# Expert stage of a decoder layer: 28 instead of 24 of 64 experts on 64 row slots, in a period of sixteen steps

## What is computed

```python
def routed_experts(xf, idx, gates, w1_e, w3_e, w2_e):
    ...
    def run_block(args):
        e, toks, g = args
        xb = xpad[toks]
        hb = jax.nn.silu(xb @ w1_e[e]) * (xb @ w3_e[e])
        return (hb @ w2_e[e]) * g[:, None].astype(xb.dtype)
    ...

def moe(x, w_router, router_bias, w1_e, w3_e, w2_e, w1_s, w3_s, w2_s):
    ...
    _, idx = lax.top_k(jnp.where(emask, biased, -jnp.inf), TOP_K)
    w_sel = jnp.take_along_axis(scores, idx, axis=1)
    gates = w_sel / jnp.sum(w_sel, axis=-1, keepdims=True) * ROUTED_SCALE
    y = swiglu(xf, w1_s, w3_s, w2_s) + routed_experts(xf, idx, gates, w1_e, w3_e, w2_e)
```

## Time and profile before

| | |
|---|---|
| median of 3 runs | 1221.01 us |
| lowest and highest | 1220.01 and 1221.2 us |
| the profiled execution's own time | 1218.57 us |
| its span (first to last instruction) | 1216.8 us |
| mean granted clock of TensorE, share of full speed | 0.978 |
| PE busy (matmuls) | 1138.4 us, 94% |
| DVE, ACT, POOL busy | 411.7, 257.2, 176.1 us |
| bytes moved by DMA | 319.16 MB |

### The profile page before, as it was taken

The page is one execution under the profiler, slowest core; times in us unless marked ns, Lnnn a source line. Parts: engine busy times, 40 slices in busy tenths (PEclk is TensorE's granted clock), DMA queues, the critical chain, the costliest instruction groups (busy, mean ns, idle before and its releaser), DMA issues.

```text
span 1216.8 us, 21054 instructions
## 1 busy us (share of the span) xinstructions
PE 1138.4 (94%) x8302; PEld 759.3 (62%) x8302; DVE 411.7 (34%) x1016; ACT 257.2 (21%) x564; POOL 176.1 (14%) x210
## 2 busy tenths in 40 slices
PE   7999997999988999889999999999999999999964
PEld 6888645877865788657755555555655555655410
DVE  0369997122048324821121212122121121111133
ACT  1101334022041125101122222122222222222200
POOL 3120050000000000111122222122221222212100
PEclk9999998999999999999999999999999999999978
DMA  9630404034047353346999999999999999999496
GB/s 332 235 139 1 156 13 173 1 138 156 1 140 258 157 209 156 155 143 243 352 384 384 385 389 384 380 386 388 388 388 380 371 381 393 384 389 385 161 367 269
DMA packets 66313, 319.16 MB, mean 262 GB/s; under 512 B 10311, under 2 KB 16671, under 8 KB 39629
## 3 DMA queue, kind: packets, MB, share of 16 engines
q1 hardware_dynamic: 51269, 278.60, 59.9%
q0 software_dynamic: 13568, 35.48, 8.6%
q10 hardware_dynamic: 1424, 4.35, 0.9%
HBM read 300.15 MB, written 29.36 MB: 271 GB/s over the span
## 4 chain that ended last, share of the span: by engine, by line
PE 72%; DVE 14%; DMA 10%; issue 1%; ACT 1%; SPq 1%; POOL 0%; POOLq 0%; DVEq 0%
PE psum L750 65%; DVE act_mem L1704 7%; PE psum L765 7%; DMA arena<-in_w_e_dram 5%; DMA arena<-y_rows 3%; DVE mk_mem L1863 2%; DMA arena<-in_w_in_dram 1%; DMA act_mem<-x_rows,idx_x 1%; SPq L541 0%; DVE act_mem L1801 0%; DVE act_mem L1718 0%; DVE rstd L1792 0%; DVE act_mem L1799 0%; DVE act_mem L1769 0%; DMA y_rows<-act_mem,idx_y 0%
## 5 line engine op out<-in xcount | busy, mean ns | idle before, releaser
L750 PE MATMUL psum<-arena,act_mem 128*32 128x128 f32 (+6 forms) x4800 | 512.3, 363 | 6.0 <-DMA arena<-in_w_e_dram 5.1
L750 PEld LDWEIGHTS psum<-arena,act_mem 128*32 128x32 f32 (+5 forms) x4800 | 263.4, 124 | 193.8 <-issue 110.7
L750 PE MATMUL psum<-act_mem,arena 128*128 128x260 f32 (+1 forms) x1728 | 352.4, 366 | 6.0 <-ACT act_mem L1550 2.0
L750 PEld LDWEIGHTS psum<-act_mem,arena 128*128 128x128 f32 x1728 | 306.0, 192 | 49.7 <-ACT act_mem L1550 2.4
L765 PE MATMUL psum<-ident,act_mem 96*128 96x96 f32 (+8 forms) x484 | 76.8, 288 | 19.3 <-POOL ident L559 6.8
L673 POOL DMA_INDIRECT y_rows<-act_mem,idx_y x40 | 45.1, 1128 | 320.2 <-DVE idx_x L2080 170.5
L2092 DVE TENSOR_SCALAR act_mem<-psum,act_mem 96x512 f32<-96x512 f32 (+1 forms) x40 | 29.9, 748 | 155.6 <-PE psum L750 155.6
L1704 DVE SCALAR_TENSOR_TENSOR act_mem<-act_mem,wcb 128x511 f32<-128x511 f32 (+29 forms) x120 | 77.7, 728 | 0.0
L765 PEld LDWEIGHTS psum<-ident,act_mem 96*128 96x128 f32 (+8 forms) x484 | 56.5, 174 | 32.3 <-issue 8.6
L2089 DVE TENSOR_TENSOR act_mem<-act_mem,psum 128x192 f32<-128x192 f32 x35 | 12.4, 354 | 175.5 <-ACT act_mem L1560 175.5
L750 PEld LDWEIGHTS psum<-act_mem 128*96 128x96 bf16 (+4 forms) x371 | 28.5, 126 | 57.2 <-issue 51.2
(11 more groups left out here) (264 smaller groups left out, 729.2 us busy)
## 6 DMA issues: line engine op xcount, KB each, us to landing
arena<-in_w_e_dram SPq DMA_DIRECT2D x192, 1024.0 KB
arena<-y_rows SPq DMA_DIRECT2D x8, 2048.0 KB, 23.5
arena<-in_w_in_dram SPq DMA_DIRECT2D x16, 512.0 KB, 18.3
arena<-in_cache_mem_k_dram SPq DMA_DIRECT2D x8, 1024.0 KB, 9.0
arena<-in_cache_mem_v_dram SPq DMA_DIRECT2D x8, 1024.0 KB, 11.8
arena<-in_w_v_dram SPq DMA_DIRECT2D x1, 4096.0 KB, 24.5
arena<-in_w_k_dram SPq DMA_DIRECT2D x1, 4096.0 KB, 13.9
arena<-in_w_out_dram SPq DMA_DIRECT2D x1, 4096.0 KB, 13.9
```

Source lines behind the costliest of these rows:

```text
L750: return pe.matmul(out, lhsT, rhs, start=first, stop=last)
```

## The change

The period becomes sixteen steps, with seven light positions: 2, 4, 6, 9, 11, 13 and 15. Over 64 steps 28 experts are on 64 slots, and four that had 96 slots now have 64. The big steps are still the long ones among the first eight positions (`BIGS`), which are now 0, 1, 3, 5 and 7. `picked`, a small tile whose size goes with NB, has a new place. The counts in the waits of `step` that were written for NB = 8 are now computed from NB. PE's, POOL's and SP's order within a step is the same, and SP's loop over the weights isn't touched; but the prologue is sixteen steps, the loop sixteen steps that run twice, and the epilogue fifteen steps.

```diff
-NB = 8
-LIGHT = (2, 5, 7)
-HEAVY = (0, 1, 3, 4, 6)
+NB = 16
+BIGS = 8
+LIGHT = (2, 4, 6, 9, 11, 13, 15)
+HEAVY = (0, 1, 3, 5, 7, 8, 10, 12, 14)
...
 def is_big(e):
-    return isinstance(e, int) and e < NB and e % NB in HEAVY
+    return isinstance(e, int) and e < BIGS and e % NB in HEAVY
 
 
 def turned(e):
 
-    return lights(e) if isinstance(e, int) and e < NB else e - (len(HEAVY) - 1)
+    return e + 1 - sum(1 for h in HEAVY if h < BIGS and (not isinstance(e, int) or h <= e))
...
-        picked = act_mem[:, A4 + 1280:A4 + 1280 + 2 * NB].rearrange("p (n c) -> p n c", c=2)
+        picked = act_mem[:, A4 + 1820:A4 + 1820 + 2 * NB].rearrange("p (n c) -> p n c", c=2)
...
             for k in HEAVY:
-                gp.memset(bump[:, NB + k:E:NB], float(CAP - MCAP)).then_inc(s_sortc, 1)
+                gp.memset(bump[:, k if k >= BIGS else NB + k:E:NB], float(CAP - MCAP)).then_inc(s_sortc, 1)
...
-                c_step(e, k % NB, 48 * (2 * i + (k // 4 + 1)))
+                c_step(e, k % NB, 48 * (NB // 4 * i + (k // 4 + 1)))
                 if exists(e + 1):
-                    b_step(e + 1, (k + 1) % NB, 16 * (2 * i + ((k + 1) // 4 + 1)))
+                    b_step(e + 1, (k + 1) % NB, 16 * (NB // 4 * i + ((k + 1) // 4 + 1)))
```

## The result

The changed kernel takes 1228.53 us (median of 7 runs, 1224.66 to 1231.22) against 1221.01 (7 runs, 1220.01 to 1222.46): a ratio of 1.0058, interval 1.0041 to 1.0075, so about 7 us slower. In a second series it was 1227.52 against 1221.83, 1.0046 (1.0028 to 1.0064). The forecast was 1219.2 with a range of 1214 to 1225.

What follows compares the result with a forecast made beforehand. Transfers were taken to bound the expert stage, PE close behind. 3.0 + 1.84 + 0.76 − 1.9 − 1.5 − 0.4 = 1.8 us gained, so 1221.0 − 1.8 = 1219.2 us, range 1214 to 1225.

Steps and rivals of the forecast that it cites:

- The bound: Expert stage: transfers limit at 9.58 us per expert, PE close behind at 9.39; PE's saved 17.1 us counts 0.
- Rival A: Expert stage: transfers keep up, wanting 404 GB/s, so PE sets the time, 1195.6 us; chance 0.06.
- cost 1: PE's longer loop: 18 to 30 more instruction pages cost 1.9 us, at most 3.8; the jump back costs 0.
- gain 1: End of the stage: the last expert's up-projection begins when the last load lands; 3.0 us gained (2.8 to 4.6).
- Rival B: Expert stage: further pages fall on few engines, making loads late; four engines 1224.8 us, one 1247.3; chance 0.12.
- Gain 2: Near the stage's start, 588 us: light position 4 closes the DMA gap before load 7; 1.84 us gained (0 to 1.84).
- Gain 3: DMA share dips after a long PE wait, at 935 to 937 and 946 to 948 us, vanish; 0.76 us gained.
- cost 2: Expert stage: PE's recurring waits for weights leave DMA dips; two episodes cost 1.5 us (0 to 4).
- Cost 3: End of the stage: c(63) waits for a landing and begins after it; 0.4 us lost (0 to 0.9).

Runs made afterwards that it cites:

- without the jump: The changed kernel with PE's loop of two passes written out, so PE never jumps back: 1222.02 us, 1.0001.
- two jumps: The kernel before with two passes of PE's loop written out as one, sixteen steps run three times: 1235.40 us, 1.0113.
- half idle engines: The changed kernel loading only a quarter of w1 and w3 and half of w2 from expert 4 on: 1199.06 us in one run.
- half of w2: The changed kernel loading only the first half of each w2 from expert 4 on: 1204.76 us, 0.9858.

## Why the prediction was wrong

**The bound: right.** The transfers set the pace. PE's 16.7 us went into waits for weights (5.1 us before, 21.2 without the jump; 10.3 + 4.7 in the first profile, beside the stall of 6.1), and came out as time only where the loads were cut. Rival A falls: in the two profiles of the changed kernel no 100 us had more than 388 GB/s, where 404 was wanted.

**The step that failed is the last sentence but two of cost 1**: "PE now has 9.58 − 9.12 = 0.46 us to spare in each step and makes up even 5 us in eleven steps, so 0". It priced the jump back as PE's time, of which there was enough. But PE also feeds the transfers: a buffer comes free when y(e) is done. PE had no lead when it stopped, since it had just waited for its weights (0.87 us before 849.16); two loads were queued, the stall and the slow clock behind it took 8.3 us, and the queue ran down. PE caught up afterwards, by waiting for nothing for some steps. The engines' idle 4.6 us can't be caught up: in the rest of the stage they are as full as before it. By the runs the jump costs 5.5 us (changed kernel against the same without it) and 5.3 each (two jumps); 2.8 between the period of sixteen with 24 light and the written-out kernel before, all within 2 us or so of uncertainty. The bound I gave it, 5 us, was near the size of the stall, and the way it would reach the time was missed.

The rule that I named there speaks of exactly this: by the Trainium skill ("Runtime: NRT & Kernel Launch", "Instruction fetch mechanics") a taken branch out of the window stalls until its page is fetched. The trace agrees: two pages moved around each of the seven stalls, and the stall was 2.1 us beside half idle engines, 4.6 to 6.1 with full loads. I had used that rule for the number of pages alone. The kernel with the loop written out fetches as many pages as the changed one (44 against 46 in 560 to 1160 us), so the second pass of a body of some 2,900 recorded instructions fetches everything again, where one of 1,517 stays for six passes.

**Cost 1, the pages: too small.** 1.9 us was taken, 3.8 was the upper bound. Alone they cost 3.2 us in time (2.0 to 4.4), and the load stretch of that one profile grew by 6.0, of which PE's lag at the end hid a part. The spread over the engines was right (2.0 us); the slower weight packets (2.0) and the idle time, mostly at the end (1.6), were not in the sum, and whether pages are their cause is open. In the changed kernel gain 1 uses up the lag that would have hidden it. Rival B is not settled: the trace doesn't say which engines carried the pages, but its prices from 5 us up are not what was measured.

**Gain 1: right in kind, 2 of 3.0 us** (c(63) 1.5 instead of 3.6 and 3.2 us behind the last packet), and one light step at the end by itself was worth 3.3 with the lighter y(62). **Gain 2: right for this order** (the gap closed and didn't move), but the reason given looked only as far as load 8: with position 4 alone light the gap came back at load 9, and position 6 being light too is what kept it shut. **Gain 3: right, cost 2: too large.** In both profiles of the changed kernel the two dips are gone, and no dip behind a wait for weights is larger than a few tenths; cost 2 took 1.5. Nor does each such wait slow what follows: behind the 2.45 us before 693.58 the long up-projection took 5.82 us, where it took 7.42 behind the 2.33 of the earlier trace rows. **Cost 3** was 1.5 (1.2 in the second profile) instead of 0.4: c(63) was held up by c(62), which had waited for its own weights 1.65 us.

The sum with the measured sizes, on the load stretch: pages 6.0, less the gap 1.8 and the dips 0.8, added to 582.5 gives 585.9, where the kernel without the jump has 585.7; with the 4.6 and 2.2 us that the engines idled behind the jump it would be 588 to 591, and the two profiles have 589.3 and 587.0. That it fits so well is partly luck: without the jump the packets' time is only 2.6 us longer than before, not 4.4, and the last 20 us fall 4.2 us short instead of 3.1. **What stays open:** by stretch and end the two profiles of the changed kernel are only 2.8 us longer than those of before (663.6 and 662.6 against 659.8 and 660.8 from the first issue), while the runs differ by 5.6 to 7.1. In the other kernels the two measures agree within about 1 us. Either the executions that were not profiled had longer stalls (the runs scatter over 10 us, from 1220.8 to 1231.2), or the stage starts later in kernels with a period of sixteen: the first issues of their six profiles lie at 558.80 to 563.03, those of the eight with a period of eight at 557.05 to 562.80, which doesn't settle it.

## What to carry to other kernels

Where the transfers set the pace, price a stall of the engine that frees their buffers by what is left in the queue, not by that engine's spare time: it has no lead, since it waits for them. A longer loop body isn't free even if its work is: look at the instruction queue in the profile to see whether the body stays between passes, and price both its pages and the jump back to it. Before speeding up all steps, look where the last of the bounding transfers lands and make only the steps behind that place faster.

## What the runs showed of the hardware

- A loop body of 1,517 recorded PE instructions is fetched once and stays for six passes; one of about 3,000 is fetched again in every pass (52 pages in 560 to 1160 us with three passes of sixteen steps, 45 with all written out, 16 with passes of eight).
- A jump back to code that had left: in seven stalls two 16 KB pages moved, and 4.3 to 4.6 us passed from the start of the first to PE's next work. With full loads that page began 0.0 to 1.7 us after PE's last work (stalls of 4.6 to 6.1 us), with half of w2 0.4 us before it (4.0), beside half idle engines 2.1 us before it (2.1).
- In a stall of 6.1 us TensorE's granted clock fell from 1.00 to 0.50 and stayed there for the next 5.3 us of work. The long up-projection behind it, 5.84 us undisturbed, took 7.9 to 8.3 us after stalls of 5.2 to 6.1 us, 7.1 after 4.6, 7.0 after 4.0 and 5.8 after 2.1. Behind waits of 1.8 to 2.5 us it took 7.4 us in some cases and 5.8 in others.
- A page of instructions took 1.07 us of one engine. 30 more of them beside full engines made the kernel 3.2 us slower (2.0 to 4.4), where their own time over 16 engines is 2.0; that the 8 KB weight packets are slower beside them (341.6 against 340.2 ns) one profile shows and another, with 43 pages and 340.5, doesn't.
